# The sample tile's expert picks split between the routing stage and the expert stage of a hybrid decoder step

## What is computed

```
qry = (xf @ w_query).reshape(T, PEER_HEADS, 2, PEER_DKEY // 2)
sa = jnp.einsum('thd,nd->thn', qry[:, :, 0], sub_keys_a)
sb = jnp.einsum('thd,nd->thn', qry[:, :, 1], sub_keys_b)
va, ia = lax.top_k(sa, PEER_TOPK)
vb, ib = lax.top_k(sb, PEER_TOPK)
...
top_s, pos = lax.top_k(cand, PEER_TOPK)
gates = jax.nn.softmax(top_s.astype(jnp.float32), axis=-1)
...
act = jax.nn.gelu(jnp.einsum('tkd,td->tk', expert_u[eb], xb), approximate=False)
return jnp.einsum('tk,tkd->td', gb * act, expert_v[eb])
```

## Time and profile before

| | us |
|---|---|
| median of 3 runs (4268.82 to 4272.81) | 4270.66 |
| the profiled execution's own time | 4266.88 |
| its span, first to last instruction | 4264.8 |
| routing, about | 1472 to 2111 |
| expert stage, about | 2111 to 4265 |

### The profile page before, as it was taken

The page is one execution under the profiler, slowest core; times in us unless marked ns, Lnnn a source line. Parts: engine busy times, 40 slices in busy tenths (PEclk is TensorE's granted clock), DMA queues, the critical chain, the costliest instruction groups (busy, mean ns, idle before and its releaser), DMA issues.

```text
span 4264.8 us, 40506 instructions
## 1 busy us (share of the span) xinstructions
PE 3624.0 (85%) x13051; PEld 2002.7 (47%) x13051; DVE 2824.8 (66%) x5382; ACT 903.9 (21%) x1895; POOL 1550.4 (36%) x1376
## 2 busy tenths in 40 slices
PE   8799977888759588887498889999999899889995
PEld 1344434555445277887344344444444444444442
DVE  1223224566433157888688898888989888987777
ACT  0111113565412014545311101110011111111110
POOL 1000000000045100000056576666766666666675
PEclk9899986888879789998699999999999999999998
DMA  8211103110155355654399899999999999999997
GB/s 322 109 47 44 49 19 135 49 50 35 23 167 154 112 193 183 252 213 164 141 368 338 330 367 381 389 346 367 377 384 391 374 382 373 350 383 396 388 382 280
DMA packets 371494, 1045.52 MB, mean 245 GB/s; under 512 B 31197, under 2 KB 106013, under 8 KB 366114
## 3 DMA queue, kind: packets, MB, share of 16 engines
q0 software_dynamic: 179728, 649.93, 40.9%
q1 hardware_dynamic: 191570, 393.17, 25.6%
HBM read 975.47 MB, written 67.22 MB: 244 GB/s over the span
## 4 chain that ended last, share of the span: by engine, by line
DVE 16%; DMA 14%; PE 7%; POOL 6%; DVEq 4%; issue 3%; ACT 0%; SPq 0%; POOLq 0%; ACTq 0%
DMA pick_v<-in_expert_v,ids 11%; DVE acc L2420 7%; DVE e_junk L2404 5%; PE psY L2303 4%; DVEq L2415 4%; POOL pick_u L2230 3%; DMA e_u<-in_expert_u 3%; POOL pick_v L2238 3%; PE psH L2290 3%; DVE e_away L1717 1%; DVE e_found L1720 1%; PE psU L2282 0%; DVE e_W L2369 0%; DVEq L1683 0%; DVE e_spare L1678 0%
## 5 line engine op out<-in xcount | busy, mean ns | idle before, releaser
L2290 PE MATMUL psH<-XT,e_uT 128*128 128x512 f32 x2048 | 968.2, 614 | 87.2 <-ACT e_uT L2327 87.2
L2303 PE MATMUL psY<-e_v,e_W 128*128 128x512 f32 x2048 | 889.2, 596 | 19.9 <-DVE e_W L2369 19.8
L2420 DVE SCALAR_TENSOR_TENSOR acc<-pick_v,pick_w,acc 128x1024 f32<-128x1024 f32 x571 | 733.4, 1284 | 243.6 <-DMA pick_v<-in_expert_v,ids 201.9
L2230 POOL DMA_INDIRECT pick_u<-in_expert_u,ids x576 | 721.6, 1253 | 391.0 <-DVE pick_dot L2404 257.6
L2238 POOL DMA_INDIRECT pick_v<-in_expert_v,ids x576 | 665.5, 1155 | 287.9 <-issue 156.4
L2404 DVE CUSTOM_DVE_ANT_0 e_junk<-pick_u,x_rows 128x1024 bf16<-128x1024 f32 x576 | 702.3, 1219 | 25.1 <-DMA pick_u<-in_expert_u,ids 12.5
L2303 PEld LDWEIGHTS psY<-e_v,e_W 128*128 128x128 f32 x2048 | 390.9, 191 | 515.5 <-issue 488.1
L2290 PEld LDWEIGHTS psH<-XT,e_uT 128*128 128x128 f32 x2048 | 381.7, 198 | 479.3 <-issue 375.5
L406 PE MATMUL ps_p<-w_in_sb,hT 128*128 128x512 f32 x1008 | 441.0, 597 | 0.0
L2327 ACT ACTIVATE e_uT<-psU 128x512 f32<-128x512 f32 x256 | 149.5, 594 | 741.8 <-PE psU L2282 741.5
L406 PEld LDWEIGHTS ps_p<-w_in_sb,hT 128*128 128x128 f32 x1008 | 190.6, 191 | 231.5 <-issue 230.8
(11 more groups left out here) (441 smaller groups left out, 4059.7 us busy)
## 6 DMA issues: line engine op xcount, KB each, us to landing
w_query_sb<-in_w_query SPq DMA_DIRECT2D x36, 2048.0 KB, 8.3
e_u<-in_expert_u SPq DMA_DIRECT2D x128, 512.0 KB, 8.0
e_v<-in_expert_v SPq DMA_DIRECT2D x128, 512.0 KB, 9.9
G_d<-G_stage SPq DMA_DIRECT2D x16, 2048.0 KB, 9.6
e_g<-G_d SPq DMA_DIRECT2D x32, 1024.0 KB, 24.9
w_ada<-in_w_ada SPq DMA_DIRECT2D x12, 2048.0 KB, 8.4
w_in_sb<-in_w_in SPq DMA_DIRECT2D x1, 14368.0 KB, 42.3
pick_u<-in_expert_u,ids POOLq DMA_INDIRECT x576, 9.0
```

The source lines that it names most:

```text
L2230: pool.indirect_dma_start(gu[:, i % NGU, :], None, io["expert_u"][0], bass.IndirectOffsetOnAxis(ids[:, q % 2, j:j + 1], 0)).then_inc(pu_in ...
L2290: m = pe.matmul(psH[a % 2][:, :], uT[:, a % 2, j, :], XT[:, j, :], start=j == 0, stop=j == KD - 1)
L2303: m = pe.matmul(psY[i % NY][:, :], W[:, (b * NBK + t) % NW, k * P:(k + 1) * P], v[:, t, half_cols(half)], start=t == 0, stop=t == NBK - 1)
L2420: dve.scalar_tensor_tensor(out=sums_q, in0=gv[:, i % NGV, :], scalar=wgt[:, m % 2, o:o + 1], in1=sums_q, op0=ALU.mult, op1=ALU.add).then_i ...
```

## The change

The sample tile is routed first (round -1) and chosen in round 0; the dense tiles 4 to 7 follow one round later each, so routing has one round more, and the last one holds only `hot` of tile 7. When the sample tile is chosen, POOL moves the halves and fetches rows for the first `QR` = 32 of its 64 double picks, first 32 times from `expert_u`, then 32 times from `expert_v`, into four buffers `r_rows`. DVE uses them in `use_row` at the end of routing's slots, paced by `rows_by`: two a slot in round 1, then one a slot. The sum stays in `acc`, now allocated outside the two stages, and the expert stage goes on with the other 32, so it has 544 picks; its pace is `tiles * 9 // 4`, 18 + 16 = 34 per eight tiles. In `hot` of tile 7 the gate is multiplied in by DVE (eight 128-column instructions) instead of ACT. `G_stage` has two buffers instead of three.

```
+    rest = [k for k in range(NT) if not is_dense(k)]
+    turns = {-1: [NT], 0: [D0, rest[0]], 1: [D0 + 1, rest[1]], ND: rest[2:], ND + 1: []}
+    for j in range(2, ND):
+        turns[j] = [D0 + j]
+    chosen = [NT] + list(range(D0, D1))
...
+    def rows_by(j, s):
+        t = max((j - 1) * SLOTS + s, 0)
+        return min(2 * max(t - 1, 0), QR) + min(max(t - QR // 2 - 4, 0), QR)
+
+    GELU = QR // 2 + 3
...
+            pool.wait_ge(made, 1)
+            pool.dma_start(ids[NS:P, 0, 0:KX // 2], c.found_i[0:NS, KX // 2:KX]).then_inc(halves_in, 16)
...
+            for n in range(2 * QR):
+                j, table = n % QR, io["expert_u" if n < QR else "expert_v"][0]
+                if n >= NR:
+                    pool.wait_ge(row_used, n - NR + 1)
+                pool.indirect_dma_start(row[:, n % NR, :], None, table, bass.IndirectOffsetOnAxis(ids[:, 0, j:j + 1], 0)).then_inc(row_in[n % NR], 16)
...
+                    if (j - 1) * SLOTS + s == GELU:
+                        act.wait_ge(row_used, QR)
+                        act.preload_act_table_set("gelu_and_others")
+                        act.activation(dot[:, :], dot[:, :], ACT.Gelu).then_inc(acted, 1)
+                        act.preload_act_table_set(EXP_LN)
...
+                if d == ND - 1:
+                    for t in range(GT):
+                        col = n * GT + t
+                        m = dve.tensor_scalar(oa[:, i % NO, t, :], number[:, :], kT[:, d % 2, 0, col:col + 1], kT[:, d % 2, 2, col:col + 1],
+                                              ALU.is_equal, ALU.mult)
+                    m.then_inc(oa_set, 1)
...
+            def use_row(n):
+
+                dve.wait_ge(row_in[n % NR], 16 * (n // NR + 1))
+                if n == 0:
+                    dve.wait_ge(xg_in, 32)
+                if n == QR:
+                    dve.wait_ge(acted, 1)
+                    dve.tensor_tensor(wgt[:, :], dot[:, :], pick_gates[:, 0, 0:QR], ALU.mult)
+                dve.drain()
+                j, r = n % QR, row[:, n % NR, :]
+                if n < QR:
+                    m = dve.tensor_tensor_reduce(acc[:, 1, :], r, xg[:, :], 1.0, 0.0, ALU.mult, ALU.add, dot[:, j:j + 1])
+                elif j == 0:
+                    m = dve.tensor_scalar(acc[:, 0, :], r, wgt[:, 0:1], None, ALU.mult)
+                else:
+                    m = dve.scalar_tensor_tensor(out=acc[:, 0, :], in0=r, scalar=wgt[:, j:j + 1], in1=acc[:, 0, :], op0=ALU.mult, op1=ALU.add)
+                m.then_inc(row_used, 1)
...
+                    while used < rows_by(j, s):
+                        use_row(used)
+                        used += 1
...
-    jobs = [(k, KX if k < NT else KX // 2) for k in JOB_TILES]
+    jobs = [(k, KX if k < NT else KX // 2 - QR) for k in JOB_TILES]
     QS = 0
+    column = lambda q, j: j + QR if q == QS else j
...
-        by_tiles = lambda tiles: tiles * 5 // 2
+        by_tiles = lambda tiles: tiles * 9 // 4
...
                 while (gelus + 1) * PB <= done:
+                    if softs < len(soft_at) and soft_at[softs] < (gelus + 1) * PB:
+                        softs += 1
+                        soften(softs)
                     pick_gelu(gelus)
                     gelus += 1
```

More of the change, by code:

```diff
@@ L1744, in routing @@
     is_dense = lambda k: D0 <= k < D1
-    rest = [k for k in range(NT + 1) if not is_dense(k)]
-    turns = {-1: [D0]}
-    for j in range(ND):
-        n = len(rest)
-        turns[j] = [D0 + j + 1] * (j + 1 < ND) + rest[j * n // ND:(j + 1) * n // ND]
-    turns[ND] = []
-    asked = [k for j in range(-1, ND + 1) for k in turns[j]]
+    rest = [k for k in range(NT) if not is_dense(k)]
[3 more added lines that the diff above has]
+    chosen = [NT] + list(range(D0, D1))
+    asked = [k for j in range(-1, ND + 2) for k in turns[j]]
     SLOTS = 16
@@ L1777, in routing @@
         gs = sb("G_stage", [P, NS_, NK, HT])
+        row = sb("r_rows", [P, NR, D])
+        dot, wgt = sb("r_dot", [P, QR]), sb("r_w", [P, QR])
         psT, psQ, psS, psG = ps("r_psT", [P, D]), ps("r_psQ", [P, 512]), ps("r_psS", [P, 512]), ps("psG", [P, 2, GT, NK])
@@ L1929, in _ @@
             done = 0
-            for j in range(-1, ND + 1):
+            for j in range(-1, ND + 2):
                 for s in range(SLOTS):
-                    if s == 0 and j >= 1:
-                        turn_picks(j - 1, done)
+                    if s == 0 and j >= 2:
+                        turn_picks(j - 2, done)
                     for i, k, at in in_turn(j, s):
                         if at == 1:
-                            if j >= 1:
-                                pe.wait_ge(kT_set, j)
+                            if j >= 2:
+                                pe.wait_ge(kT_set, j - 1)
                             turn(i)
@@ L1943, in _ @@
                             score(i, at - 3)
[L1944 to L1945 removed]
+                    if j >= 2:
+                        spread((j - 2) * SLOTS + s)
         @block.scalar
@@ L2398, in dot_pick @@
                 q = job_of(i)
-                if i == first[q]:
-                    dve.wait_ge(xg_in, 16 * (q + 2))
+                if i == first[q] and q >= 1:
+                    dve.wait_ge(xg_in, 16 * q)
                 dve.wait_ge(pu_in[i % NGU], 16 * (i // NGU + 1))
@@ L2416, in spend_pick @@
                 sums_q = acc[:, q % 2, :]
-                if i == first[q]:
+                if i == first[q] and q != QS:
                     dve.tensor_scalar(sums_q, gv[:, i % NGV, :], wgt[:, m % 2, o:o + 1], None, ALU.mult).then_inc(spent, 1)
```

173 lines of the change are left out of this document (90 added, 83 removed).

## The result

| | before | after |
|---|---|---|
| median (range), us | 4269.74 (4266.59 to 4272.81) | 4318.27 (4314.06 to 4321.51) |
| the profiled execution's own time | 4266.88 | 4319.15 |
| its span | 4264.8 | 4317.3 |

The change makes the kernel slower: ratio 1.0119, 95% interval 1.0107 to 1.0132. The prediction was 4274 us, with a range up to 4297. Between the two spans lie 52.5 us, and three points of both traces divide them: the first query of routing on PE, the end of the last `hot` on DVE, and the first `psH` matmul of the expert stage.

The account below looks back on a forecast made before the run. DVE was taken to bound routing; in the expert stage, PE under `sums` and DMA in tile parts. Routing +74 and expert stage -71 gave +3, 4266.9 to 4270; with 3.8 for the median, 4274 us, range 4254 to 4297.

Parts of the forecast that it names:

- step (1): Routing: 64 row instructions on DVE at 1.33 us each, 85 us, covered by nothing except the waits.
- step (2): Routing, DVE's pieces of a round: choice 64 us, `hot` 39, a tile's norm and copy 5, plus rows.
- Rounds -1 and 0 stay as they are: Routing's start: three tiles' queries on PE as before, sample tile chosen instead of tile 4, ending near 1611.5.
- Step (4): Routing's round 5, `hot` alone: DVE 39 to 48 us, PE 33 to 56, taken as 45.
- Step (5): Expert stage's twelve pairs: two picks fewer in each DMA-bound tile part, 5.3 us each, 60 us saved in all.
- Step (6): Expert stage's first stretch: choice of job 1 within 32 picks instead of 64; -11 us, bounds -17 and +7.
- rival B: Expert stage's first `sums`: DVE's picks delay ACT's gelu and copies, PE stops; +7 for -11, 4292 us, chance 0.20.
- Step (7): Expert stage's last tile part and everything from 4162 on: no change.
- Rival C: Routing: DVE waits for fetched rows; at 16 us per fetch round 1 gives +45, 4319 us, chance 0.08.
- Rival D: Expert stage: relieved by the full 89 us because DVE is freed too; -18, 4256 us, chance 0.22.

Follow-up runs that it names:

- order_only: The changed kernel with no rows used in routing, all 64 double picks in the expert stage at the old pace: 4304.88 us, ratio 1.0084.
- experiment 4: Kernels with other pace, fetch buffers, routing rows or `e_u` loads, mostly against the changed kernel: ratios 1.0020 to 1.0092, single executions 4336.69 to 4466.20 us.
- experiment 2: The changed kernel with all rows still fetched in routing but DVE's products over them left out: 4274.59 us, one execution.

## Why the prediction was wrong, point by point

**Routing, nearly right in its sum, by two errors that cancel, which is luck.** From the end of round 0 to the last `hot` the forecast was 559 us, and 563.6 were measured (1617.1 to 2180.7): rounds of 116, 129, 130, 125 and 45 us and 14 at `kT` against 120.6, 131.2, 133.0, 127.1 and 51.7 with the `kT` waits in them. DVE's waits, 5 + 14, were 20.4. But step (1), "Nothing covers it, except the waits", failed: the 64 rows cost 51 us, for round 1 had 37 us in which DVE was idle, 24 of them in waits for ACT and PE. And the pieces of step (2), without the rows and their changes to the waits, make the new order 11 us shorter, where it is 38 longer: my round 1 without rows was 64 + 10 + 5 us of DVE, and PE's two tiles make it 102.6. With the rows DVE comes near to PE's time, which is why the sum came out.

**"Rounds -1 and 0 stay as they are"** was short by 5.6 us: the first search starts 30.8 us after the first query instead of 19.8, and only a first query 5.2 us earlier hid half of it. That too is luck: on the chip of `order_only`, with nothing changed ahead of routing, the first query came between 1481.9 and 1489.3 us. The 11 us are PE's clock. Before the first query it was granted at 0.50 in both kernels; the kernel before came up to the higher level (2.4 GHz) within the first queries, but while PE works on the sample tile's, of 64 columns, it stays at 0.51, the lower level (1.2 GHz). First query to first search before, then after; under each window PE's timeline of its two groups of 64 matmuls:

```profile
1488.50:1508.30 19.80, 19.02 (x143) 18.81 (x144) 1.23 (x2) 1.79 (x3) 0.00 (x0) 0.86 0.48 175
1488.48 10.10 PE L1899 MATMUL r_psQ<-XT,w_query_sb 128*128 128x128 f32 x64 [0.88 <-DVE XT L2048]
1499.36 7.38 PE L1899 MATMUL r_psQ<-XT,w_query_sb 128*128 128x128 f32 x64 [0.78 <-ACT qT L1968]
...
1483.30:1514.10 30.80, 30.23 (x144) 30.08 (x144) 1.23 (x2) 1.36 (x3) 0.00 (x0) 0.51 0.43 152
1483.30 13.88 PE L1919 MATMUL r_psQ<-hT_g,w_query_sb 128*128 128x64 f32 x64 [0.61 <-DVE hT_g L2081]
1497.75 13.89 PE L1919 MATMUL r_psQ<-hT_g,w_query_sb 128*128 128x64 f32 x64 [0.56 <-ACT qT L1990]
```

Every kernel with the new order has these 30.8 us.

**Step (4)** was mis-sized: 51.7 us for 45, inside its bounds of 39 to 56. PE's clock was granted at 0.93, but eight 128-column instructions take 2.14 us from the first one's start, above my upper bound of 1.8. Timeline of DVE at the start of round 5:

```profile
2129.65 2.14 DVE L2095 TENSOR_SCALAR hot_a<-number,kT 128x128 f32<-128x128 f32 x8
2131.70 1.23 DVE L2101 TENSOR_TENSOR hot_b<-number,kT 128x1024 f32<-128x1024 f32 x1
```

**Step (5), the expert stage, is the step that failed most:** "Two picks fewer per eight tiles, both in the tile part of a pair". The twelve pairs gave 29.9 us, not 60. The rate was right, the place wrong: the tile parts lost 0.5 MB each and not 2.1, 1.4 us and not 5.3. In the runs of experiment 4 the bytes moved from part to part with the `e_u` buffers and the order of issue at one pace, so it is how far the queues can run ahead, and not the pace table alone, that sets which part a saved byte leaves. `after_early_u` shows the other half: with a fourth `e_u` buffer and an earlier issue its tile parts take 69.5 us, near the 73.7 - 5.3 = 68.4 that the step implies. The Trainium skill (DMA: Bandwidth & Descriptors, Specifications) names about 358 GB/s as HBM's limit for a core; in no kernel was the mean of the `sums` parts above 353, but the mean of the tile parts was 381 to 396 in all, so in this kernel that figure is not the limit.

**Step (6) failed, and rival B's mechanism came true** near its price: +4.8 us for the first stretch, where B said +7 and the forecast -11. I had pick 32 at 152 us behind the first dot and the point of decision near 170; it came at 168.6 (2205.1 and 2373.7), a hair short of it, and ACT and PE stopped as B describes. By parts the stretch took 81.7, 67.8, 101.3, 54.9 and 71.2 us, where step (6) has 83, 68, 72, 55 and 78 in its other way of adding up: tile part two, which holds the stop, is 29 us over, and no other part is longer than that forecast. Timelines of ACT, then of PE:

```profile
2360.70 0.21 ACT L2392 ACTIVATE pick_dot<-pick_dot 128x8 f32<-128x8 f32 x1 [37.23 <-DVE pick_dot L2465]
...
2402.95 0.21 ACT L2392 ACTIVATE pick_dot<-pick_dot 128x8 f32<-128x8 f32 x1 [32.37 <-DVE pick_dot L2465]
```

```profile
2404.19 3.72 PE L2351 MATMUL psH<-XT,e_uT 128*128 128x512 f32 x4 [26.49 <-ACT e_uT L2388]
```

The gelu of eight picks waits on ACT for DVE, ACT's copies of `e_uT` stand behind it, and PE behind these. The stop is one tile part later than B had it: the gelu of picks 24 to 31 cost ACT 37.2 us, most of it while PE ran `sums`, and the next one cost PE 26.5 us. That first `sums` part was longer by 12.9 us for another reason, which also comes from the crowded DVE: PE waited for DVE to add `psY` to `Y`.

```profile
PE psY L2364 <- DVE Y L2436: 10.0, 2, 8.1
```

With 48 picks in place of 32 (`qr16`) PE waits 9.8 us for `e_uT` in the whole first stretch, which takes 369.3 us.

**Step (7)**, nothing, was 3.9 us on the good side. **Rival C** fell: rows landed after 4.1 to 14.0 us, median 5.5, and DVE never waited for them. Its neighbour did cost: the fetches hold up PE's `w_query` loads in round 1 (experiment 2). **Rival D**, a full relief of 89 us, did not come: with early `e_u` loads the expert stage takes 2083.6 us, 58 below before.

In all, the spans differ by 52.5 us where the working had 3. Of the 49.5 us between, 7.5 are routing's, 15.8 the first stretch's, 30.1 the pairs', and -3.9 what comes behind them.

What stays open: why the clock stays at its lower level through the sample tile's queries, and why round 0 of the same routing takes 103 us in some executions and 111 in others, at a lower clock.
